# Moving the folds of the modulation's partial sums behind VectorE's work for each output block, and folding the sums of three seams too

## What is computed

```
for l in range(DEPTH):
    m  = (sc  @ w_mod[l] + b_mod[l])      # 9 x 1024, modulation of the latent tokens
    mc = (scc @ w_mod[l] + b_mod[l])      # 9 x 1024, modulation of the context tokens
    h = h + 0.5 * m[2] * swiglu(modulate(h, m[0], m[1]), w_ff1_in[l], w_ff1_out[l])
    h = h + m[5] * mixer(modulate(h, m[3], m[4]))
    h = h + 0.5 * m[8] * swiglu(modulate(h, m[6], m[7]), w_ff2_in[l], w_ff2_out[l])
    # the context stream runs through the same weights with mc
```

## Time and profile before

| | |
|---|---|
| time, median of 3 | 3354.51 us (3353.33 to 3356.08) |
| profiled execution, its own time | 3355.72 us |
| its span in the trace | 3353.9 us |
| TensorE busy | 3210.7 us (96%) |
| VectorE busy | 1606.9 us (48%) |
| ScalarE busy | 964.9 us (29%) |
| granted TensorE clock, mean | 0.981 |

### The profile page before, as it was taken

One profiled execution on the slowest core, in us unless ns is written; L12 is line 12 of the kernel. 1 busy time (PEld: TensorE's weight loads), 2 busy tenths in 40 slices (PEclk: granted clock), 3 DMA queues, 4 the chain that ended last, 5 costly groups with the idle time before them and its releaser, 6 DMA issues.

```text
span 3353.9 us, 44374 instructions
## 1 busy us (share of the span) xinstructions
PE 3210.7 (96%) x18259; PEld 2896.2 (86%) x18259; DVE 1606.9 (48%) x2348; ACT 964.9 (29%) x1453; POOL 267.0 (8%) x316
## 2 busy tenths in 40 slices
PE   5999999998999999899999999999999998999999
PEld 5999999986669894488999999999999976678887
DVE  7754526424542636636724354532225547743333
ACT  3211212356441321133212112311212345632222
POOL 1100000200001005620000001000000100000000
PEclk8999999999999999999999999999999999999999
DMA  5533424401004220014523243232224220023332
GB/s 196 171 101 101 125 70 135 135 25 55 1 1 132 63 63 1 1 39 125 150 64 96 73 126 90 86 88 65 66 65 141 60 63 14 1 82 98 97 95 94
DMA packets 381726, 272.91 MB, mean 81 GB/s; under 512 B 17410, under 2 KB 357625, under 8 KB 381433
## 3 DMA queue, kind: packets, MB, share of 16 engines
q1 hardware_dynamic: 356217, 182.50, 18.7%
q0 software_dynamic: 25344, 88.09, 8.4%
HBM read 262.16 MB, written 8.39 MB: 81 GB/s over the span
## 4 chain that ended last, share of the span: by engine, by line
PE 89%; ACT 4%; DVE 3%; issue 2%; POOL 1%; DMA 1%; SPq 0%; ACTq 0%; DVEq 0%
PE ps L458 74%; PE ps L1251 1%; PE ps L1372 1%; PE ps L700 1%; PE ps L1146 1%; PE ps L1226 1%; PE ps L1232 1%; PE ps L1242 1%; PE ps L1742 1%; ACT gpt L1404 1%; PE ps L1776 1%; PE ps L1743 1%; PE ps L1049 1%; PE ps L1759 1%; PE ps L1749 1%
## 5 line engine op out<-in xcount | busy, mean ns | idle before, releaser
L458 PE MATMUL ps<-u_hi,w_hi 128*128 128x384 f32 (+2 forms) x2992 | 827.4, 346 | 18.5 <-DVE u_lo L599 13.5
L458 PE MATMUL ps<-u_hi,w_lo 128*128 128x384 f32 (+2 forms) x2992 | 820.7, 344 | 0.0
L458 PE MATMUL ps<-u_lo,w_hi 128*128 128x384 f32 (+2 forms) x2992 | 820.7, 344 | 0.0
L448 DVE TENSOR_TENSOR w_lo<-ring,w_hi 128x1024 fp32r<-128x1024 f32 (+3 forms) x357 | 415.5, 1165 | 843.3 <-ACT w_hi L433 649.1
L458 PEld LDWEIGHTS ps<-u_hi,w_hi 128*128 128x128 f32 x2992 | 541.1, 189 | 46.5 <-issue 22.7
L458 PEld LDWEIGHTS ps<-u_lo,w_hi 128*128 128x128 f32 x2992 | 541.6, 189 | 22.4 <-issue 1.7
L458 PEld LDWEIGHTS ps<-u_hi,w_lo 128*128 128x128 f32 x2992 | 540.8, 189 | 21.1
L433 ACT CAST w_hi<-ring 128x1024 fp32r<-128x1024 f32 (+3 forms) x229 | 221.6, 969 | 1011.3 <-PE ps L458 965.1
L458 PE MATMUL ps<-hid_hi,w_hi 128*128 128x384 f32 (+1 forms) x1232 | 340.6, 346 | 10.1 <-DVE w_lo L448 10.1
L458 PE MATMUL ps<-hid_lo,w_hi 128*128 128x384 f32 (+1 forms) x1232 | 339.5, 345 | 0.0
L458 PE MATMUL ps<-hid_hi,w_lo 128*128 128x384 f32 (+1 forms) x1232 | 339.1, 344 | 0.0
(11 more groups left out here) (267 smaller groups left out, 3347.2 us busy)
## 6 DMA issues: line engine op xcount, KB each, us to landing
ring<-in_w_ff_in SPq DMA_DIRECT2D x176, 512.0 KB, 3.9
m_in<-in_w_mod POOLq DMA_DIRECT2D x128, 512.0 KB, 4.0
ring<-in_w_ff_out SPq DMA_DIRECT2D x64, 512.0 KB, 3.6
ring<-in_w_in_e SPq DMA_DIRECT2D x26, 512.0 KB, 3.8
ring<-in_w_ff_out SPq DMA_DIRECT2D x32, 384.0 KB, 3.1
m_first<-in_w_mod POOLq DMA_DIRECT2D x16, 512.0 KB, 12.9
ring<-in_w_out_e SPq DMA_DIRECT2D x16, 512.0 KB, 3.8
ring<-in_w_in_o SPq DMA_DIRECT2D x12, 512.0 KB, 3.7
```

The source lines that it names most:

```text
L448: dve.tensor_tensor(w_lo[:, b:b + WIDE[n]], ring[:, s:s + WIDE[n]], w_hi[:, b:b + WIDE[n]], ALU.subtract).then_inc(w_split_lo, 1)
L458: mm = pe.matmul(ps_at(p, c0, c1) if halved else pair(p)[:, c0:c1], w, x[:, c0:c1], start=start and i == 0, stop=stop and i == 2)
```

## The change

The fold leaves `dve_mod_piece` and goes to `dve_out_ff`: in the output phase, at step x = 1, 2, 3 for the first, second and third job of the part, behind the split of weight chunk x (and at x = 1 behind `hid_lo`). The two jobs of each of the three seam parts are folded too, at x = 1 and x = 2 of the output phase of their part, and `pe_norm` sums them with `pe_mod_halves` instead of `pe_mod`. `SEAM_BANKS` gives the PSUM banks of the two halves; VectorE waits for the last job of the seam before it reads the first.

```diff
--- before.py
+++ after.py
@@ -365,7 +365,7 @@
                 (2, 0): [(5, 2)], (2, 2): [(5, 1), (5, 0)]}
         NORM_BY = {R_FF(0, 2): 1, R_SSD: 2, R_FF(1, 2): 3, R_FF(2, 2): 4, R_GQA: 5}
         MODS_AT = {1: (0, 2), 3: (1, 2), 4: (2, 2)}
-        SEAM_BANK = {1: 4, 3: 2, 4: 4}
+        SEAM_BANKS = {1: (4, 5), 3: (2, 3), 4: (4, 5)}
         JOBS = [(0, 1), (0, 0)] + [x for key in sorted(MODS) for x in MODS[key]]
         JOB = {x: i for i, x in enumerate(JOBS)}
 
@@ -559,7 +559,7 @@
             mm.then_inc(n_ss, 1)
             if n in MODS_AT:
                 for slot_, job in enumerate(MODS[MODS_AT[n]]):
-                    pe_mod(pe, job, slot_, mods_used(*MODS_AT[n]), SEAM_BANK[n])
+                    pe_mod_halves(pe, job, slot_, SEAM_BANKS[n])
 
         def dve_norm(dve, n):
             for c in range(2 if n else 0):
@@ -575,8 +575,9 @@
                 if q > 0:
                     dve_low(dve, n, NORM_RUN[n], q - 1)
                 if q == 6 and n in MODS_AT:
+                    dve.wait_ge(m_mm, JOB[MODS[MODS_AT[n]][-1]] + 1)
                     for slot_, job in enumerate(MODS[MODS_AT[n]]):
-                        dve_mod(dve, job, slot_, SEAM_BANK[n])
+                        dve_mod(dve, job, slot_, SEAM_BANKS[n])
 
         def dve_scale(dve, n, run, d):
             t = NORM_T[n]
@@ -660,11 +661,8 @@
                 dve.wait_ge(m_mm, first)
             dve.wait_ge(m_full[n % 2], 16 * ((n - n_first) // 2 + 1))
             m_add(dve, m_in[:, D * (n % 2):D * (n % 2) + D], k, slot_)
-            if k == DB - 1 and x in HALVED:
-                dve.wait_ge(m_used, n + 1)
-                dve_fold(dve, x, slot_)
-
-        HALVED = [x for key in sorted(MODS) if key not in MODS_AT.values() for x in MODS[key]]
+
+        HALVED = [x for key in sorted(MODS) for x in MODS[key]]
 
         HALF_BANKS = ((4, 7), (5, 6), (4, 7))
 
@@ -676,10 +674,10 @@
             dve.tensor_tensor(m_sum[64:128, e:e + D], m_sum[0:64, e:e + D], m_sum[64:128, e:e + D],
                               ALU.add).then_inc(m_fold, 1)
 
-        def pe_mod_halves(pe, x, slot_):
+        def pe_mod_halves(pe, x, slot_, banks=None):
 
             pe.wait_ge(m_fold, HALVED.index(x) + 1)
-            top, low = HALF_BANKS[slot_]
+            top, low = banks or HALF_BANKS[slot_]
             if slot_ == 2:
                 pe.wait_ge(mod_raw, JOB[x] - 1)
             for d in range(DB):
@@ -701,15 +699,16 @@
                                    ones[:, 0:1], start=True, stop=True)
             mm.then_inc(m_mm, 1)
 
-        def dve_mod(dve, x, slot_, first=4):
+        def dve_mod(dve, x, slot_, banks=None):
 
             g, q = x
             other = x in HALVED
             if other:
-                top, low = HALF_BANKS[slot_]
-                first = top - slot_
+                top, low = banks or HALF_BANKS[slot_]
+            else:
+                top = 4 + slot_
             dve.wait_ge(m_mm, JOB[x] + 1)
-            raw = bank(first + slot_, 16 * q, 16 * q + 16).rearrange("p (d s) -> p d s", s=2)
+            raw = bank(top, 16 * q, 16 * q + 16).rearrange("p (d s) -> p d s", s=2)
             m = mod_group(g)
             for s in range(2):
                 y = dve.scalar_tensor_tensor(out=m[:, q, :, s], in0=raw[:, :, s] if not other or not s else
@@ -903,6 +902,9 @@
                     dve.wait_ge(f_hi, FH[i_f, part] + nk)
                     dve.tensor_tensor(hid_lo[:, nk - 1, :t], hid_f[:, q, :t], hid_hi[:, nk - 1, :t],
                                       ALU.subtract).then_inc(f_lo, 1)
+                if 1 <= x <= len(MODS.get((i_f, part), [])):
+                    dve.wait_ge(m_used, mods_used(i_f, part))
+                    dve_fold(dve, MODS[i_f, part][x - 1], x - 1)
                 jobs = [] if last else MODS.get((i_f, part), [])
                 if jobs and x == 2:
                     dve_mod(dve, jobs[0], 0)
```

## The result

The changed kernel takes 3331.77 us (median of 4 runs, 3330.62 to 3335.95) where the kernel before takes 3354.89 us beside it (4 runs, 3353.33 to 3356.08). The ratio is 0.9933, with a 95% interval of 0.9921 to 0.9944: 22.5 us less (the medians by themselves differ by 23.1). A second set of runs on another chip gave the same ratio (experiment 9). The profiled execution's own time is 3330.62 us, its span 3328.8 us against 3353.9, so 25.1 us less in the traces.

What follows compares the result with a forecast made beforehand. TensorE, with 89% of the span, bounds the kernel: its matmuls plus its waits. Part ends 13.3 plus seams 8.8, 22.1 us off 3355.72, give 3333.6 (3332.4 against the median), stated as 3333; range 3326 to 3344.

Steps and rivals of the forecast that it cites:

- Part ends, 13.3 us: Ahead of output block 0 in (0,0) and (1,0): TensorE's waits on `w_lo` and the slow block vanish, 13.3 us.
- the slow block: Output block 0 behind the long wait, at the lower clock: 10.02 us against 8.55; 1.47 us should go.
- The folds hidden, 0 us: In the output phases: the moved folds fit into VectorE's room and cost nothing, with 0.5 us left at the tightest place.
- rival that the folds come onto the path (3371): In the output phases: 16 folds of 2.44 us lengthen the path, 39.0 us less 22.1, so 3371; chance 0.04.
- The seams, 8.8 us: In three seams: sums hide in TensorE's idle time, so block 6 begins 3.48, 1.86 and 3.47 us sooner, together 8.8.
- The reason given for this, that VectorE sets the pace behind the start: In the seams: TensorE reaches block 6 at VectorE's pace, as in norm 2's seam; reason for the 8.8 us.
- The term's unequal parts: Gains claimed for the three seams up to block 6: 3.48, 1.86 and 3.47 us.
- The clock behind the sums: Behind output-phase sums: clock drops to 1.2 GHz, 1.6 us each, fall by chance; their number left as it is.
- rival of a drop behind every sum (14 us more): In the output phases: all ten sums have a clock drop, 14 us more, 3347; drops beyond the likeliest range, chance 0.10.
- The sum: Whole kernel: 13.3 us at part ends plus 8.8 in seams, 22.1 us less.
- The rival that only half pays: Part ends or seams give less: 3341 without the seams, 3346 without the part ends; chance 0.13.
- that another wait takes over (3354): At output block 0: another wait replaces the one removed, so nothing happens, 3354; chance 0.03.

Runs made afterwards that it cites:

- experiment 9: The changed kernel timed again, unaltered, on another chip: 3335.68 us, ratio 0.9934 to the kernel before.
- experiment 4: Also called two_in_place: the changed kernel with first and second folds back behind their last pieces in the two three-job parts; 3338.3 us, ratio 0.9951.
- experiment 5: The changed kernel with two more additions (2.45 us) behind the fold at x = 2 in the three seam parts; 3339.35 us, ratio 0.9949.
- experiment 6: The changed kernel with only the first of eight column blocks of each job summed in the three seams; 3333.2 us, ratio 0.9927.
- experiment 7: The changed kernel with `dve_mod` moved from ahead of block 6 to behind the seam's loop of blocks; 3336.1 us, ratio 0.9941.
- experiments 1 and 2: Changed kernel in halves: first, only output-phase folds moved, seams keep whole sums, 3345.74 us; second (seams_only), only the seams changed, 3345.43 us.
- experiment 10: The changed kernel with the ten output-phase jobs folded again, to 32 partitions, and summed in four row groups; 3321.81 us, ratio 0.9895.

## Why the prediction was right, step by step

**The time**: 3333 forecast, 3331.77 measured, and 3335.68 in experiment 9. That the first is within 1.3 us is partly luck, since one run differs from the next by up to 7 us.

**Part ends, 13.3 us**: the traces show 6.80 + 6.58 = 13.4, and by itself it measured 12.1 by the ratio. The chain of steps held: `hid_lo` 190.0 to 190.9, an accumulation, then the last one bound by its load (forecast from 194.8, found at 194.00), `w_lo` ended at 197.6 (forecast 198.5), 2.0 us ahead of block 0 (forecast 1.6), and all of the wait went, with the slow block behind it. The granted clock was 1.00 ahead of the wait's end and 0.57 from 205 to 209 us, and experiment 4 shows that it was the answer to this long wait: behind one half as long block 0 took 8.49 us, and 8.41 without a wait.

**The folds hidden, 0 us**: right, and it was as tight as said: 0.5 us of room forecast, 0.37 found, 0.4 to 0.6 by experiment 5. The rival that the folds come onto the path (3371) has a real threshold, but one that this change stays just short of: in the changed kernel no product waits for an addition to `h`.

**The seams, 8.8 us**: 3.36 + 1.66 + 3.35 = 8.37 in the traces, 9.4 (within its interval of 5.4 to 13.4) by itself. The sums do hide in TensorE's idle time, and that is confirmed by experiment 6. The size was read from where TensorE would begin block 6, and there it begins within 0.3 us of VectorE's row in all three seams. The reason given for this, that VectorE sets the pace behind the start, is only half of it: experiment 7 takes VectorE's work ahead of block 6 away, and TensorE, slow by its clock, comes there at most 0.3 us sooner. That the two bounds lie so close was not in the prediction; the size is right partly by this coincidence. The term's unequal parts (1.86 for norm 3, 3.48 and 3.47 for the others) are one execution's clock, as said above.

**The clock behind the sums**: left as a spread of some 1.6 us each, and that is what it was: three, three and five drops in the traces of the kernel before and of the changed one, taken twice. Its rival of a drop behind every sum (14 us more) counted one drop before; there were three, so it would have been some 11 us. That both profiled executions had three is luck. Not foreseen was the drop of 2.8 us in the state-space stage, which the prediction had not looked at. It made the two profiled executions differ by more than the medians.

**The sum**: 22.1 us forecast, 21.7 found in the places named, 22.5 by the ratio. The rival that only half pays is ruled out by experiments 1 and 2, each of which is faster than before by more than its interval; that another wait takes over (3354) by the rows of block 0.

## What to carry to other kernels

A wait on TensorE's path is shortened by moving what stands ahead of the late producer on its engine. Count its work up to the moment when TensorE asks: here one fold of three was nearly free, the second was worth 2.6 us, and the third 2.5 us and a slow block. Work that is moved needs a place with room for all of it. This room is the time from the end of the last piece of work there to the start of the matmul that waits for it (here from the addition of block 0 to block 2).

Where TensorE is idle anyway, making its small sums shorter gives nothing (experiment 6); where it is not, a job of one-column matmuls costs its own length and, now and then, the clock behind it. There the way is to fold further on an engine with room, as experiment 10 does.

Two profiled executions can differ by some us in places that the change never touches. Set the same matmuls side by side before an unexpected gain is explained, and before a forecast is read from one trace: a seam that looks shorter than its likes may have had the better clock.

## What the runs showed of the hardware

**The clock behind short sums goes by chance, by place and by their length.** In ten traces of kernels whose sums take 1.88 us there are 29 drops behind 100 sums, each worth some 1.6 us. The first sum of (1,0) has one in all ten traces, the first of (0,0) in six, of (0,1) in five, of (2,0) in three and of (1,1) in one; second sums have four of 30, and third sums none of 20. In the two traces whose ten sums take 0.31 or 0.99 us there are none behind 20. Two windows of the changed kernel, ahead of the first sum of (0,0) and behind it:

```profile
200.00:208.00 8.00, 8.00 (x47) 7.78 (x45) 5.31 (x5) 1.66 (x2) 0.00 (x0) 1.00 0.22 67
...
210.00:214.50 4.50, 4.50 (x17) 4.50 (x18) 4.35 (x9) 0.00 (x0) 0.00 (x0) 0.62 0.31 91
```

TensorE is busy throughout both, and its clock is 1.00 in the one and 0.62 in the other, which over 4.5 us is 3.4 us at 1.2 GHz. The Trainium skill (TensorE: Matmul & The Clock Gate, What's actually happening) says that the window in which activity is looked at runs freely, and is not started by the work. That the drops come and go at most of these sums agrees with it. Why first sums are hit most often, and the one of (1,0) every time, this doesn't explain, and no run here shows it. Sums of 0.99 us had no drop behind them ten times; what lies between 0.99 and 1.88 us no run here shows.

**The answer to a wait isn't proportional.** Behind 5.04 us of idleness ahead of block 0 the first row was at 1.2 GHz at all four places in two traces (before and seams_only). Behind 2.43 us, at both places of two_in_place, it was not. Nor is the price behind the long wait fixed: block 0 took 10.02 and 9.79 us in the one trace and 11.08 and 9.80 in the other, against 8.41 without a wait, so 1.4 to 2.7 us.

**Four row groups.** A job's sum takes 1.88 us with two row groups of 64 rows and 0.99 us with four of 32 rows, each time as 32 matmuls of the trace. The Trainium skill (TensorE: Matmul & The Clock Gate, Part 3: Packing small matmuls) says that matmuls at tile positions with other rows of the array run at once. These two figures agree. So do the starts: by halves two matmuls start 0.01 us apart and the next two 0.11 us later, and in experiment 10 four start within 0.02 us and the next four 0.11 us later. The first two of a sum by halves:

```profile
208.03 0.27 PE L686 MATMUL ps<-cst,m_sum 64*128 64x1 f32 x1
208.04 0.27 PE L687 MATMUL ps<-cst,m_sum 64*128 64x1 f32 x1
```
